# Combining stage of a two-layer decoder trunk: LayerNorm scale and bias rows requested after the sample tile's rows instead of after all rows

## The reference, cut to what matters

```python
def _layer_norm(x, g, b):
    xf = x.astype(jnp.float32)
    mu = jnp.mean(xf, axis=-1, keepdims=True)
    var = jnp.mean(jnp.square(xf - mu), axis=-1, keepdims=True)
    return ((xf - mu) * lax.rsqrt(var + LN_EPS) * g + b).astype(x.dtype)

def _post_norm(x, sub, g, b):
    return _layer_norm(DN_ALPHA * x + sub, g, b)     # DN_ALPHA = 4 ** 0.25
```

## Time and profile before

| what | us |
|---|---|
| median of three runs | 1393.95 |
| lowest, highest of the three | 1393.51, 1405.43 |
| the profiled execution, its own time | 1396.67 |
| its span, first to last instruction | 1394.9 |
| combining stage of layer 0, first load issued to last copy of ACT | 632.25 to 675.97 |
| combining stage of layer 1, first load issued to the end of the span | 1350.70 to 1394.9 |

### The profile page before, as it was taken

How to read it: one execution, slowest core, us unless ns; L and a number is a source line. 1 busy time by engine, 2 the same in 40 slices (tenths; PEclk the granted TensorE clock), 3 DMA queues, 4 the chain that set the end, 5 groups by cost and what they waited for, 6 DMA issues and landing times. The chain is left out here.

```text
span 1394.9 us, 15206 instructions
## 1 busy us (share of the span) xinstructions
PE 1122.1 (80%) x5745; PEld 568.8 (41%) x5745; DVE 482.1 (35%) x1308; ACT 249.2 (18%) x529; POOL 192.7 (14%) x184
## 2 busy tenths in 40 slices
PE   7999999499799777880499998985997998878540
PEld 5865666355633222220243344543555333222110
DVE  3515665366611111115221333541766111111017
ACT  0311333111111111112111212241111111111011
POOL 0000000000011111003243542220000111111112
PEclk9999999799899999895599998996998999999775
DMA  6510100293579999944676997664915899999723
GB/s 255 192 63 1 61 1 1 104 406 128 211 293 420 420 420 420 421 198 177 264 278 243 394 361 273 242 249 154 421 57 213 344 418 420 420 421 420 312 92 145
DMA packets 84851, 360.41 MB, mean 258 GB/s; under 512 B 13858, under 2 KB 18083, under 8 KB 54819
## 3 DMA queue, kind: packets, MB, share of 16 engines
q1 hardware_dynamic: 60802, 276.47, 49.7%
q0 software_dynamic: 19808, 74.48, 13.9%
q10 hardware_dynamic: 4160, 8.39, 1.6%
HBM read 344.90 MB, written 31.16 MB: 270 GB/s over the span
## 5 line engine op out<-in xcount | busy, mean ns | idle before, releaser
L1660 PE MATMUL e_psum_g<-m_wg,top_xT 128*64 128x512 f32 x1056 | 264.7, 652 | 71.9 <-DMA m_wg<-in_moe_w_gate_up 69.2
L1660 PEld LDWEIGHTS e_psum_g<-m_wg,top_xT 128*64 128x64 f32 x1056 | 80.9, 149 | 246.7 <-issue 159.7
L1684 PE MATMUL e_psum_y<-m_wd,top_xT 128*64 128x512 f32 x528 | 123.4, 610 | 5.4 <-DMA m_wd<-in_moe_w_down 3.4
L1253 PE MATMUL n_psum_p<-m_wg,top_xT 128*128 128x512 f32 x256 | 117.5, 606 | 0.0
L1714 DVE COPY top_xT<-e_psum_x 128x512 f32<-128x512 f32 x33 | 22.8, 692 | 214.2 <-PE e_psum_x L1645 214.2
L1154 POOL DMA_INDIRECT m_xg<-token_rows,m_tokof x33 | 33.5, 1016 | 456.6 <-PE e_psum_x L1645 241.7
L1951 PE MATMUL cd_psum_ab<-cd_w,top_xT 128*128 128x512 f32 x192 | 86.4, 603 | 0.0
L475 PE MATMUL ab_psum<-ab_w,top_xT 128*128 128x512 f32 x192 | 85.2, 597 | 0.0
L1800 POOL DMA_INDIRECT cd_kv<-in_cache_kT,top_kpages x64 | 62.0, 968 | 98.5 <-PE cd_psum_d L1993 44.3
L460 PE MATMUL ab_psum<-top_xT,ab_w 128*128 128x272 f32 x320 | 73.9, 393 | 1.0 <-DMA ab_w<-in_ab_w_in 1.0
L1723 DVE TENSOR_SCALAR e_Y<-e_psum_y,m_share 128x512 f32<-128x512 f32 x33 | 24.8, 751 | 129.0 <-PE e_psum_y L1684 129.0
(11 more groups left out here) (432 smaller groups left out, 1438.1 us busy)
## 6 DMA issues: line engine op xcount, KB each, us to landing
m_wg<-in_moe_w_gate_up SPq DMA_DIRECT2D x128, 1024.0 KB, 25.9
m_wd<-in_moe_w_down SPq DMA_DIRECT2D x64, 1024.0 KB, 25.7
cd_kv<-in_cache_kT SPq DMA_DIRECT2D x64, 256.0 KB, 7.2
ab_w<-in_ab_w_in SPq DMA_DIRECT2D x4, 2048.0 KB, 7.6
m_wg<-expert_rows SPq DMA_DIRECT2D x16, 512.0 KB, 7.6
cd_w<-in_cd_w_in ACTq DMA_DIRECT2D x4, 2048.0 KB, 13.8
m_wg<-in_ab_w_out SPq DMA_DIRECT2D x2, 2048.0 KB, 10.6
token_rows<-top_X SPq DMA_DIRECT2D x8, 512.0 KB, 3.8
```

Of the source, the lines that this page charges most:

```text
L1253: last = nc.tensor.matmul(pp[(2 * i + h) % 3][:P, :], mixT[:, k, tok0(t):tok0(t) + P], w[h][:, k, :], start=(k == 0), stop=(k == KD - 1))
L1660: last = nc.tensor.matmul(pg[i % 2][64 * a:64 * a + 64, :], xgT[i % 2][:, j, 64 * a:64 * a + 64], wg[2 * (i % NR) + a][:, j * 512:(j + 1) ...
L1684: last = nc.tensor.matmul(py[n2][64 * a:64 * a + 64, :], hT[:, j, 64 * a:64 * a + 64], wd[2 * (i % NR) + a][:, j * D + n2 * 512:j * D + (n ...
```

## The change

The two requests for the scale and bias rows move from behind the loop over the tiles to inside it, behind the sample tile's two loads. The sample tile is number 4 and comes first. Nothing else is changed; both layers use the function.

```diff
                 for k in range(2):
                     row = ROWS * k + tok0(t)
                     sp.dma_start(y[t][:P, k, :], y_dram[row:row + P, :]).then_inc(y_in[t], 16)
-            sp.dma_start(gb[:, 0, :], lng.partition_broadcast(128)).then_inc(gb_in, 16)
-            sp.dma_start(gb[:, 1, :], lnb.partition_broadcast(128)).then_inc(gb_in, 16)
+                if t == 4:
+                    sp.dma_start(gb[:, 0, :], lng.partition_broadcast(128)).then_inc(gb_in, 16)
+                    sp.dma_start(gb[:, 1, :], lnb.partition_broadcast(128)).then_inc(gb_in, 16)
             for i, (t, P) in enumerate(ORDER):
                 sp.wait_ge(final, i + 1)
```

## The result

The changed kernel takes 1404.46 us (median of 20 runs), the kernel before, run beside it, 1397.53 us (20 runs). The ratio is 1.0042, 95% interval 1.0023 to 1.0061, which is 3.2 to 8.5 us slower. A second measurement on another chip gave 1.0045 (1.0023 to 1.0066). So the change makes the kernel slower, by less than 1%.

What follows compares the result with a forecast made beforehand. DVE's wait for the bias row in both layers' combining stages was taken as the bound. A direct gain of 4.5 us against a meeting costing 4.0 to 4.1 us a layer gave 1393.95 + 3.6 = 1397.6 us, range 1388.5 to 1401.5.

Steps and rivals of the forecast that it cites:

- What bounds the stage: Both layers' combining stages: DVE idles 4.80 us (layer 1) and 4.95 us (layer 0) before the affine, awaiting the bias row.
- The slip of two places: SP's load queue: the prompt tiles' rows land later by 2.53 us in layer 1 and 2.66 us in layer 0.
- The direct gain: Sample tile's first affine starts 2.25 us earlier in layer 1 and 2.26 us in layer 0, -4.5 us in sum.
- The meeting of POOL and DVE: POOL's adds of p1 to p3 and DVE's two-input steps block each other, costing 4.0 to 4.1 us a layer.
- The sum: Both layers' stages together: 1.76 us later in layer 1 and 1.85 us in layer 0, +3.6 us.
- The absolute time: Whole kernel: median 1393.95 us plus 3.6 us gives 1397.6 us, +0.26%.
- A: Combining stages: POOL alone gives way, DVE runs on unstopped; -4.5 us, 1389.4 us, up to 1390.0; chance 0.28.
- B: Combining stages: POOL's add doesn't get between DVE's scale product and bias add; +0.35 us, 1394.3 us; chance 0.15.
- C: Load queue's head: broadcast rows come at 300 GB/s, add(p0) slips 1 us more per layer; chance 0.07 together with D.
- D: Combining stages: prompt rows wait as long as DVE was idle, no effect, 1393.95 us; chance 0.07 together with C.

Runs made afterwards that it cites:

- run 11: No run label: the third of three runs of the unchanged kernel, at 1405.43 us; 11 is its distance in us from the other two.

## Why the prediction was right or wrong

**What bounds the stage: right.** The bias row's landing was the wait, and both layers' stages count: each is longer or shorter as the table shows, and the ratios of the kernels with scale and bias in PSUM need the gains of both. POOL's adds were off the path before (-0.9 us when they are left out).

**The slip of two places: right in kind, sized too small.** Forecast 2.53 and 2.66 us. POOL's add of p0 began 6.92, 7.53, 6.35 and 7.65 us behind the first issue in the four stages of before, 10.67, 9.42, 10.55 and 10.13 us in those of the changed kernel: means 7.11 and 10.19, a slip of 3.1 us. The distance between p0 and p1 in one profile was too low a price, and single stages scatter by over 1 us, which one profile doesn't show. Why it is 0.5 us more stays open. The price of 2.5 us is the full stretch's 414 GB/s, but the rows now stand at the head of the queue, and the first 6 us there go at 219 to 250 GB/s in the four stages of the changed kernel; 1.05 MB in 3.1 us would be 340 GB/s. Against this as the whole cause: in the two kernels without POOL's adds p0's residual began 6.91 and 7.35 us behind the first issue with the rows late, 9.34 and 9.71 with them early, a slip of 2.4 us, at 242 and 244 GB/s in those first 6 us. The direct gain was 2.0 us a layer (the first affine at 15.47 instead of 17.47 us, means of four), not 2.25.

**The meeting of POOL and DVE: right.** The forecast was 4.0 to 4.1 us a layer; the steps lost 4.25. The forecast's 13.40 us between POOL's start on p0 and the end of p1's residual stand against 13.46, 13.45, 13.45 and 13.44 in the four stages. The forecast's L251 (1367.65 to 1370.89, 3.24 us) takes 3.24 or 3.25 us in the four stages. The Trainium skill (page SBUF — State Buffer, section "SBUF: two separate sides") has whichever of the two starts first hold the shared pair of ports for its whole instruction. The traces agree, on DVE's side now with stops of up to 2.2 us in place of 0.1 us.

**The sum: direction right, size too small.** Forecast +3.6 us, the stages +4.1 and +4.7. Per layer 0.25 us of direct gain and 0.1 to 0.2 us of meeting are missing, 0.8 us in both. (The larger slip moves the first affine by only 0.25 us against the forecast, because the forecast had started from one profile with a p0 0.1 us later than the mean, and because the affine follows POOL's start on p0 by 5.3 us, not 5.4.) The ratios say +5.9 (3.2 to 8.5) and +6.3 us (3.2 to 9.3); the stages lie inside both intervals, and whether the other 1.7 us are scatter or something outside the stages the runs leave open. The stretch between the two stages shows no such cost: it is 674.7 and 682.3 us long in the two profiles of before, 672.0 and 677.6 in those of the changed kernel, a scatter far above 1.7 us.

**The absolute time: wrong. Here is the step that failed.** The sum was 1393.95 + 3.6 = 1397.6, and its first term was mis-sized: the median of three runs was 1393.95, the median of twenty is 1397.53. 3.6 of the 6.9 us by which 1404.46 lies above the forecast are this. The other 3.3 us are in the second term, the change: forecast +3.6 us, measured +6.9 as the difference of the two medians (+5.9 by the ratio, +4.1 and +4.7 by the stages). The range had covered the first term with "the scatter of a median; the three runs' lower two lie 0.4 us apart". With the third run 11 us above them the scatter was in plain sight. The same range around 1397.53 would have ended at 1405.1 and held the measured time. That the direction came out right isn't luck: the steps of DVE that the prediction named are the ones that grew, by 4.25 us a layer where it had worked out 4.0 to 4.1.

**Rivals.** A (DVE isn't stopped) falls: DVE's steps lose 4.25 us a layer. B (POOL doesn't get in between L250 and L251, 0.03 us apart) falls: the second of them takes 3.24 or 3.25 us in all four stages. C (broadcast rows slow at the head) is neither shown nor excluded: it priced the slip at 3.5 us, the forecast at 2.5 to 2.7, and 3.1 lies between. The 413 GB/s are of the stretch behind these rows and say nothing about them. The first 6 us are at 219 to 250 GB/s, and with ordinary rows in that place at 233 to 268. The means, of six stages each and the kernels without POOL's adds counted in, are 240 and 253. That is 0.08 MB less in 6 us, by an estimate 0.2 us at 414 GB/s, and may be a part of the 0.5 us. D (no effect) falls.

## What to carry to other kernels

An idle wait can be a cover: before moving the transfer that ends it, look at what the other engines do inside it, and whether their instructions can run beside the ones that will take its place. Where POOL and DVE both read tiles in SBUF, look at how single instructions overlap. Give DVE's step one operand in PSUM, or place POOL's work by a wait behind a two-input step of DVE, so that it falls on steps with one input. A stage's length read from several profiles settles a few us that the run times can't, and a median of three is no base when the third run lies 11 us from the other two.

## What the runs showed of the hardware

- A DVE step with two inputs in SBUF and a POOL add, both of 128x1024 or 32x1024 f32, hold each other off for a whole instruction, whoever is in first: DVE's 1.21 us became up to 3.38 and 3.30 us, POOL's 2.33 us became 3.1 to 3.3 us. The one that waited ends 1.07 us (DVE) or 2.20 us (POOL) after the other.
- A waiting POOL add takes a gap of 0.03 us between two such steps of DVE, in all four stages of the changed kernel; cut into halves of 1.26 us, one half goes in, not the whole add.
- DVE's statistics, which read one tile, take 1.29 us beside a POOL add and don't lengthen it.
- With the second input in PSUM the DVE step takes 1.21 us beside a POOL add.
- Which of the two is first hung on 0.03 to 0.11 us, so that one kernel's two layers differed by 2.2 us in a step.
